# GpSimd sums the squares of the new x at the seam to the first layer

## The reference, cut to what matters

```python
# end of the first block
h_lat = h_lat + gate_l[:, None] * rms_norm(y @ w_out, post_w)
# beginning of the second block, layer 0
h = _rmsnorm(x, attn_norm_g[l])        # x is h_lat; x * rsqrt(mean(x * x) + EPS) * g
proj = h @ w_in[l]
q, k, v, gate_b, gate_c, conv_in = jnp.split(proj, splits, axis=-1)
```

## Time and profile before

| What | Value |
|---|---|
| Median of three runs | 3031.68 us (3027.84 to 3032.13) |
| Span of the profiled execution (the page gives no other time for it) | 3030.7 us |
| TensorE matmul busy | 2988.4 us, 99% |
| VectorE / ScalarE / GpSimd busy | 61% / 44% / 6% |
| Seam: first update of x starts | 858.50 us |
| Seam: last matmul over ones ends | 881.30 us |

### The profile page before, as it was taken

How to read it: one execution, slowest core, us unless ns; L and a number is a source line. 1 busy time by engine, 2 the same in 40 slices (tenths; PEclk the granted TensorE clock), 3 DMA queues, 4 the chain that set the end, 5 groups by cost and what they waited for, 6 DMA issues and landing times.

```text
span 3030.7 us, 68077 instructions
## 1 busy us (share of the span) xinstructions
PE 2988.4 (99%) x28670; PEld 2825.7 (93%) x28670; DVE 1853.3 (61%) x2510; ACT 1333.4 (44%) x1731; POOL 192.4 (6%) x287
## 2 busy tenths in 40 slices
PE   5999999999999999999999999999999999999999
PEld 2688888888999999999999999999999999999999
DVE  3677777688876666555455555566665555555554
ACT  3455555455454444444343333444444443333333
POOL 0000000000100001110010000100012110000000
PEclk8999999999999999999999999999999999999999
DMA  9712212323955444555555555544445555555554
GB/s 392 280 58 85 85 58 85 117 100 113 392 196 202 175 179 171 191 194 193 191 193 192 192 193 194 221 178 170 177 170 187 192 192 194 193 193 194 194 194 152
DMA packets 82964, 547.13 MB, mean 181 GB/s; under 512 B 9125, under 2 KB 13365, under 8 KB 18928
## 3 DMA queue, kind: packets, MB, share of 16 engines
q1 hardware_dynamic: 78448, 523.27, 47.1%
q10 hardware_dynamic: 2192, 15.40, 1.3%
q0 software_dynamic: 2160, 6.05, 0.6%
HBM read 540.46 MB, written 7.36 MB: 181 GB/s over the span
## 4 chain that ended last, share of the span: by engine, by line
PE 96%; DVE 1%; DMA 1%; PEld 0%; ACT 0%; issue 0%; PEldq 0%; SPq 0%; ACTq 0%; DVEq 0%
PE bank L443 29%; PE bank L444 28%; PE bank L445 28%; PE bank L845 1%; PE bank L712 1%; PE bank L718 1%; DMA raw<-stream 1%; PE bank L948 1%; PE bank L754 1%; DMA xr<-x_t 1%; PE bank L1150 0%; PE bank L770 0%; PE bank L931 0%; PE bank L771 0%; PE bank L772 0%; PE bank L956 0%
## 5 line engine op out<-in xcount | busy, mean ns | idle before, releaser
L422 ACT CAST w_hi<-raw 128x2048 fp32r<-128x2048 f32 x443 | 846.7, 1911 | 1226.3 <-PE bank L445 1226.2
L427 DVE TENSOR_TENSOR w_lo<-raw,w_hi 128x2048 fp32r<-128x2048 f32 x443 | 1017.6, 2297 | 550.7 <-ACT w_hi L422 550.6
L443 PE MATMUL bank<-a_lo,w_hi 128*128 128x256 f32 (+1 forms) x3568 | 1061.1, 297 | 0.6 <-DVE w_lo L2078 0.3
L444 PE MATMUL bank<-a_hi,w_lo 128*128 128x256 f32 (+1 forms) x3568 | 1035.5, 290 | 0.0
L445 PE MATMUL bank<-a_hi,w_hi 128*128 128x256 f32 (+1 forms) x3568 | 1035.2, 290 | 0.0
L443 PE MATMUL bank<-h_lo,w_hi 128*128 128x256 f32 x3552 | 990.5, 279 | 3.8 <-DVE h_lo L2114 3.8
L444 PE MATMUL bank<-h_hi,w_lo 128*128 128x256 f32 x3552 | 981.6, 276 | 0.0
L445 PE MATMUL bank<-h_hi,w_hi 128*128 128x256 f32 x3552 | 981.4, 276 | 0.0
L443 PEld LDWEIGHTS bank<-a_lo,w_hi 128*128 128x128 f32 x3568 | 672.0, 188 | 24.6 <-DVE g_X L1884 2.8
L445 PEld LDWEIGHTS bank<-a_hi,w_hi 128*128 128x128 f32 x3568 | 671.3, 188 | 17.2
L444 PEld LDWEIGHTS bank<-a_hi,w_lo 128*128 128x128 f32 x3568 | 670.9, 188 | 12.2
(11 more groups left out here) (353 smaller groups left out, 2128.5 us busy)
## 6 DMA issues: line engine op xcount, KB each, us to landing
raw<-stream SPq DMA_DIRECT2D x485, 1024.0 KB, 4.8
gate_raw<-stream ACTq DMA_DIRECT2D x12, 1024.0 KB, 7.6
xr<-x_t SPq DMA_DIRECT2D x4, 1024.0 KB, 16.4
q_raw<-stream SPq DMA_DIRECT2D x8, 512.0 KB, 10.0
x_res<-x_t SPq DMA_DIRECT2D x1, 2048.0 KB, 16.2
bias_table<-bias SPq DMA_DIRECT2D x1, 2048.0 KB, 10.9
bias<-bias_table ACTq DMA_DIRECT2D x1, 2048.0 KB, 10.8
out_t<-x_res SPq DMA_DIRECT2D x4, 512.0 KB, 5.1
```

Source lines behind the costliest of these rows:

```text
L422: act.copy(w_hi[u.slot][:], raw[u.raw][:]).then_inc(hi_ready, 1)
L427: dve.tensor_tensor(w_lo[u.slot][:], raw[u.raw][:], w_hi[u.slot][:], ALU.subtract).then_inc(lo_ready, 1)
L443: pe.matmul(acc, wh, lo[:, k, 0:n], start=(k == first), stop=False)
L444: pe.matmul(acc, wl, hi[:, k, 0:n], start=False, stop=False)
```

## The change

On GpSimd a new stretch clears `n_acc`, and then adds 15 of the 16 squares to it, one by one as ScalarE makes them. ScalarE makes square k right behind `weighted_hi(k)`, into `n_sq` and `n_ln` in turn, and from k = 2 on waits for the addition of square k-2. TensorE no longer does a matmul over ones for each square: after k = 15 it does `norm_sums(1)`, one for the sum and one for the last square.

```diff
--- before.py
+++ after.py
@@ -675,6 +675,15 @@
             pool.wait_ge(S["bias_table"], 48)
             pool.dma_start(*diagonals(TABLE_HEADS, HEADS)).then_inc(S["bias_table"], 16)
 
+            pool.wait_ge(S["ss_mm"], 1)
+            own.link(pool.memset(n_acc[:], 0.0))
+            for s in range(KT - 1):
+                pool.wait_ge(S["x_sq"], s + 1)
+                if s:
+                    pool.wait_ge(S["x_sq_used"], s)
+                m = pool.tensor_tensor(n_acc[:], n_acc[:], (n_sq, n_ln)[s % 2][:], ALU.add)
+                m.then_inc(S["x_sq_used" if s < KT - 2 else "acc_ready"], 1)
+
             for e in range(2, 1 + 2 * LAYERS):
                 pool.wait_ge(S["ss_mm"], e)
                 own.add(pool.memset(n_acc[:], 0.0))
@@ -1081,12 +1090,12 @@
                 unit_mm(pe, Unit(U_WOUT + 7, i), y_hi3, y_lo3, L, part=(12, KT))
 
             def norm_sums(e):
-                pe.wait_ge(S["acc_ready"], e + 1 - (e > 1))
+                pe.wait_ge(S["acc_ready"], e + 1)
                 mm(psum[2][:, 0:L], ONES, n_acc[:], start=True, stop=False)
-                if e == 0:
-                    pe.wait_ge(S["mo_sq"], KT)
-                mm(psum[2][:, 0:L], ONES, n_sq[:] if e else hbuf[:, 3 * L:4 * L], start=False, stop=True
-                   ).then_inc(S["ss_mm"], 1)
+                if e < 2:
+                    pe.wait_ge(S["x_sq" if e else "mo_sq"], KT)
+                last = (hbuf[:, 3 * L:4 * L], n_ln[:])[e] if e < 2 else n_sq[:]
+                mm(psum[2][:, 0:L], ONES, last, start=False, stop=True).then_inc(S["ss_mm"], 1)
 
             def first_normed(u, e, second=None):
 
@@ -1099,10 +1108,7 @@
                 for k in range(KT):
                     unit_mm(pe, u, h_hi3, h_lo3, L, ready, part=(k, k + 1))
                     unit_mm(pe, second, h_hi3, h_lo3, L, part=(k, k + 1))
-                    for s in (*((k - 3, k - 2) if k % 2 and k > 2 else ()), *((k - 1, k) if k == KT - 1 else ())):
-                        pe.wait_ge(S["x_sq"], s + 1)
-                        mm(psum[2][:, 0:L], ONES, (n_sq, n_acc)[s % 2][:], start=(s == 0), stop=(s == KT - 1)
-                           ).then_inc(S["x_sq_used" if s < KT - 1 else "ss_mm"], 1)
+                norm_sums(1)
 
             norm_sums(0)
             for l in range(LAYERS):
@@ -1564,12 +1570,11 @@
                 if l == 0:
                     for k in range(KT):
                         weighted_hi(0, 0, k)
-                        for s in (*((k - 3, k - 2) if k % 2 and k > 2 else ()), *((k - 1, k) if k == KT - 1 else ())):
-                            if s >= 2:
-                                act.wait_ge(S["x_sq_used"], s - 1)
-                            f((n_sq, n_acc)[s % 2][:], x_res[:, s * L:(s + 1) * L], ACT.Square).then_inc(S["x_sq"], 1)
-                            if s == KT - 3:
-                                split_act_half(Unit(U_LAYER + 2), 0)
+                        if k >= 2:
+                            act.wait_ge(S["x_sq_used"], k - 1)
+                        f((n_sq, n_ln)[k % 2][:], x_res[:, k * L:(k + 1) * L], ACT.Square).then_inc(S["x_sq"], 1)
+                        if k == KT - 2:
+                            split_act_half(Unit(U_LAYER + 2), 0)
                     split_act_half(Unit(U_LAYER + 2), 1)
                 norm_root(1 + 2 * l)
                 if l:
```

## The result

The changed kernel takes 3040.81 us in the median (3039.82 to 3041.08, 5 runs), the kernel before 3030.51 beside it (3027.84 to 3032.13, 5 runs): 10.3 us more, a ratio of 1.0037 with a 95% interval of 1.0026 to 1.0049 (the two medians alone give 1.0034). Forecast were 3042.8 us, and slower.

A forecast was written before the change was run, and what follows sets the result against it. TensorE's chain was taken to bound the kernel, with VectorE at the same pace at the seam. Late start 4.6, toll 5.4 and clock 1.1 sum to 11.1 us on the median 3031.68: 3042.8, range 3034.5 to 3047.5.

The forecast's parts named there:

- VectorE as the second bound: At the seam VectorE keeps TensorE's pace, 1.13 us a tile against 1.15, so relieving TensorE gives only 0.02 per tile.
- The late start: GpSimd's additions start at about 868.2, behind the second bias DMA, delaying ScalarE and VectorE; with the tail, +4.6 us.
- the old wait of 0.85: At the seam VectorE once waited 0.85 us for ScalarE; the prediction said this wait no longer occurs.
- the changed tail: After tile 14's update at 881.4, ScalarE does a half cast before the last high part; sums end at 885.87.
- The toll on VectorE: At the seam twelve additions, 2 to 13, each cost VectorE's two-input instructions 0.45 us: +5.4 us, bounds 0 and 8.9.
- TensorE's clock: After the new wait TensorE may end the seam's loop at 1.2 GHz; half of 2.2 us taken, +1.1.
- Slipping between VectorE's instructions: Rival: at the seam additions fit VectorE's gaps, only the late start counts: 3036.3 us, or 3037.4 with clock; chance 0.19.
- whole additions: Rival: at the seam VectorE stands for whole additions and the clock ends low: 15.7 us more, 3047.4; chance 0.12.
- GpSimd in time: Rival: bias DMA lands before about 859, nobody waits at the seam: 3029.2 us, or 3034.6 with toll; chance 0.05.

The follow-up runs named there:

- The seam with neither loss: Changed kernel with GpSimd's second bias DMA moved behind the 15 additions and each addition replaced by a clearing of the same buffer: 3027.22 us, ratio 0.9990.
- The clearings: Changed kernel with each of the 15 additions replaced by a GpSimd clearing of the same buffer, same late start: 3034.62 us, ratio 1.0015.
- A copy: Changed kernel with each addition replaced by a GpSimd copy of the square, reading one SBUF tensor instead of two: 3034.13 us in one execution.
- the two experiments that made it so: Changed kernel with the second bias DMA behind the GpSimd work: 3027.22 us with clearings instead of additions, 3034.57 us with additions kept.
- rounded squares: Kernel before, with squares and the ones of their matmuls in fp32r on TensorE, GpSimd doing nothing new: 3028.09 us, ratio 0.9992.
- four buffers and the early half cast: Kernel before with rounded squares, four square buffers instead of two, and the third unit's first half cast ahead of the first tile: 3025.12 us, ratio 0.9987.

## Why the prediction was right, point by point

- **VectorE as the second bound.** Right. The seam with neither loss is 21.37 us, only 2.4 under the kernel before, though TensorE has 6 us less to do there.
- **The late start.** Right in place and mechanism, a little small. The low part of tile 3 started 862.94 - 857.57 = 5.37 us into the seam before and 867.41 - 854.30 = 13.11 after, 7.7 later; the sum had 7.0. The sum took over the distance from the first gated update to the second bias DMA, 866.97 - 857.57 = 9.40 us; in the changed kernel's trace it is 864.54 - 854.30 = 10.24, which accounts for it. Less the old wait of 0.85 and with the changed tail, the term was +4.6 and came out at 7.74 - 0.85 - (5.97 - 4.61) = +5.5. Here 5.97 and 4.61 are the tails, from the end of the update of tile 14 to the end of the sums.
- **The toll on VectorE.** Right: twelve instructions as counted. From the low part of tile 3 to the update of tile 14 went 884.87 - 867.41 = 17.46 us, 5.9 over the 11.54 of the sum, against +5.4. That is 0.49 an addition instead of 0.45. The clearings take the toll away with the same waits and signals; they read nothing, but they are also shorter (0.31). A copy, which reads and is hardly longer when nothing holds it up (0.40), brings a part of it back, so the toll comes with the reading. The Trainium skill (SBUF — State Buffer, section "Who interferes with whom") says that a GpSimd instruction that only writes does not contend with VectorE's two-input instructions, and one that reads SBUF does. Clearings, copies and additions agree. Not whole instructions are lost, though: 0.5 us for an addition of 0.72 to 0.94, and 0.14 for a copy of 0.40 to 0.62.
- **TensorE's clock.** The term that was mis-sized. The sum had +1.1, half of the price of ending at 1.2 GHz, because the earlier trace rows could not tell at which level the loop ends. The granted clock was 0.50 from 868 to 876, with TensorE busy for 7.01 of 8.00 us, and 1.00 from 877 to 888, with 6.95 of 11.00. The clock went up and stayed up, so this term was 0.
- **The sum.** 5.5 + 5.9 + 0 = 11.4 in the profiles, as the seam's 11.45, against 11.1 forecast; 10.3 in the medians. That forecast and seam lie so close is in part luck: two terms were too small, by 0.9 and 0.5, and the clock's was too large by 1.1. Of the 2.0 us by which 3042.8 is above the measured 3040.81, 1.2 come from the start of the sum, the median of three runs (3031.68), where the median of five is 3030.51.
- **The rivals.** Slipping between VectorE's instructions fell with the twelve long ones, whole additions with 0.49. The 2.66 of the earlier trace rows had been counted for whole additions, but there GpSimd stood and not VectorE: the addition at 1174.61 began during a VectorE instruction that ran until 1176.69 (row below), and ended 0.58 after it. GpSimd in time was priced at 2.5 us under the kernel before without the toll and 2.9 over it with the toll (3029.2 and 3034.6); the two experiments that made it so gave 2.95 under and 4.4 over (3027.22 and 3034.57). That the second time was met is luck: the price had a toll of 5.4 on a kernel before of 3031.68, and measured were 7.1 (fourteen additions) and 3030.17.

The VectorE instruction beside the addition at 1174.61, from VectorE's timeline of the kernel before:

```profile
1174.11 2.58 DVE L427 TENSOR_TENSOR w_lo<-raw,w_hi 128x2048 fp32r<-128x2048 f32 x1 [0.96 <-ACT w_hi L422]
```

## What to carry to other kernels

Work moved to an engine that looks idle starts where that engine's program stands, not where the work is ready: look for what its queue waits for at that moment. If two engines keep the same pace, relieving one gave little here beyond the tail and one wait (2.4 of 6 us), and a helper whose reads slow the other one makes that the new bound. Making the work itself cheaper where it stood (rounded squares) came out 2 us under the kernel before, not clear of the scatter, and 4 us under it with four buffers and the early half cast; moving it lost 10.

## What the runs showed of the hardware that was not expected

- A GpSimd addition of 128 x 256 cost VectorE's two-input instructions 0.51 us in the mean of fourteen, a copy 0.14, a clearing nothing. The additions themselves were held up by little: they lasted 0.94 at the most in the changed kernel, against 2.66 in the earlier trace rows.
- TensorE's clock in the changed kernel went up to 2.4 GHz after a stretch of 8.00 us at 1.2 GHz in which the engine was busy for 7.01, and was still up at the end of a stretch of 11.00 us in which it was busy for 6.95.
